# Decode tile with high and low halves in one stationary tile, and layer norms with summed squares on ScalarE

## The reference, cut to what matters

```python
x = _layer_norm(DN_ALPHA * x + 0.5 * _swiglu(x, f1g, f1u, f1d), ln_g[0], ln_b[0])
m, s_new, new_k, new_v = _mixer(x, w_in, w_out, gn_w, sinks, ret_state, k_buf, v_buf)
x = _layer_norm(DN_ALPHA * x + m, ln_g[1], ln_b[1])
x = _layer_norm(DN_ALPHA * x + 0.5 * _swiglu(x, f2g, f2u, f2d), ln_g[2], ln_b[2])
```

## Time and profile before

| | us |
|---|---|
| median of 3 runs | 2297.51 (2296.41 to 2300.42) |
| profiled execution, its own time | 2296.21 |
| its span, first to last instruction | 2294.4 |
| TensorE busy | 2216.7 |
| VectorE busy | 949.5 |
| GpSimd busy | 515.3 |
| ScalarE busy | 452.6 |

### The profile page before, as it was taken

The page is one execution under the profiler, slowest core; times in us unless marked ns, Lnnn a source line. Parts: engine busy times, 40 slices in busy tenths (PEclk is TensorE's granted clock), DMA queues, the critical chain, the costliest instruction groups (busy, mean ns, idle before and its releaser), DMA issues. The chain is left out here.

```text
span 2294.4 us, 31139 instructions
## 1 busy us (share of the span) xinstructions
PE 2216.7 (97%) x12117; PEld 1998.7 (87%) x12117; DVE 949.5 (41%) x1580; ACT 452.6 (20%) x799; POOL 515.3 (22%) x253
## 2 busy tenths in 40 slices
PE   8999999999999989999898899899999999999996
PEld 8999999999999889996676458799999999999995
DVE  5434434344344550012133546634343443434347
ACT  4111111111111221111123540211111111111111
POOL 4121121212212222212122522221212122121213
PEclk9999999999999999999697699999999999999998
DMA  7101011010111011110103030010110101011011
GB/s 267 56 27 55 27 55 53 29 55 27 55 47 45 37 61 65 37 35 17 65 10 138 0 125 1 19 55 28 55 51 31 55 27 55 29 53 55 28 56 78
DMA packets 37817, 118.39 MB, mean 52 GB/s; under 512 B 5879, under 2 KB 10615, under 8 KB 37503
## 3 DMA queue, kind: packets, MB, share of 16 engines
q1 hardware_dynamic: 37759, 117.58, 14.4%
HBM read 106.29 MB, written 11.27 MB: 51 GB/s over the span
## 5 line engine op out<-in xcount | busy, mean ns | idle before, releaser
L111 PE MATMUL bank<-x_hi,f_w_hi 128*128 128x362 f32 (+1 forms) x2104 | 689.3, 328 | 7.7 <-issue 6.4
L113 PE MATMUL bank<-x_hi,f_w_low 128*128 128x362 f32 (+1 forms) x2104 | 689.5, 328 | 0.0
L362 POOL TENSOR_TENSOR f_w_low<-f_w_raw,f_w_hi 128x1024 fp32r<-128x1024 f32 x132 | 316.8, 2414 | 1199.2 <-ACT f_w_hi L288 1199.2
L534 DVE TENSOR_TENSOR acc<-bank,acc 128x512 f32<-128x512 f32 x756 | 500.5, 689 | 15.2 <-PE bank L461 6.9
L514 DVE TENSOR_TENSOR f_h_full<-bank,f_silu 128x362 f32<-128x362 f32 (+1 forms) x132 | 70.7, 536 | 817.4 <-PE bank L113 815.0
L111 PEld LDWEIGHTS bank<-x_hi,f_w_hi 128*128 128x128 f32 x2104 | 396.4, 188 | 10.0 <-issue 8.1
L113 PEld LDWEIGHTS bank<-x_hi,f_w_low 128*128 128x128 f32 x2104 | 396.7, 189 | 0.0
L112 PE MATMUL bank<-x_lo,f_w_hi 128*128 128x362 f32 (+1 forms) x1056 | 346.2, 328 | 0.0
L112 PE MATMUL bank<-x_low,f_w_hi 128*128 128x362 f32 (+1 forms) x1048 | 342.8, 327 | 0.0
L442 PE MATMUL bank<-f_w_hi,f_h_lo 128*128 128x512 f32 x720 | 281.8, 391 | 0.0
L443 PE MATMUL bank<-f_w_low,f_h_hi 128*128 128x512 f32 x720 | 281.5, 391 | 0.0
(11 more groups left out here) (165 smaller groups left out, 2209.9 us busy)
## 6 DMA issues: line engine op xcount, KB each, us to landing
f_w_raw<-ffn_in SPq DMA_DIRECT2D x132, 512.0 KB, 4.5
rp_w_raw<-w_ret_in SPq DMA_DIRECT2D x16, 512.0 KB, 3.5
acc<-x_rows_in SPq DMA_DIRECT2D x2, 2048.0 KB, 11.0
kept_rows<-acc SPq DMA_DIRECT2D x8, 512.0 KB, 2.6
ow_raw<-w_out_in SPq DMA_DIRECT2D x8, 512.0 KB, 11.1
y_out<-acc SPq DMA_DIRECT2D x8, 512.0 KB, 2.6
n_rows<-ln_rows_in SPq DMA_DIRECT2D x6, 512.0 KB, 7.9
gp_stage<-w_att_in SPq DMA_DIRECT2D x6, 512.0 KB, 3.5
```

Of the source, the lines that this page charges most:

```text
L111: pe.matmul(out, wh, xh, start=first, stop=False)
L113: return pe.matmul(out, wl, xh, start=False, stop=last)
L362: pool.tensor_tensor(flat(w_lo[s][j]), flat(w_raw[s][j]), flat(w_hi[s][j]).bitcast(F32), ALU.subtract).then_inc(done, 1)
L534: dve.tensor_tensor(acc[r, t, d], down_ps[(n + 2 * s) % 4][r, :], acc[r, t, d], ALU.add).then_inc(down_free, 1)
```

## The change

**Decode tile in the feed-forward stages.** `h_hi` gets 128 more columns: 64 for the low part of the decode tokens, right behind their high part, and 64 zeros. One stationary tile of 128 columns now holds high and low part, so two matmuls (with the high and the low weights) replace three; the bank's rows 0 to 63 hold the high part's product and rows 64 to 127 the low part's. `acc` keeps both apart in the decode tile over the loop (rows 64 to 127 start at zero), and `last_down` folds them with a matmul by `fold`, two 64x64 identities above each other, in full f32.

**Order.** In `last_down`, the norms and the output projection, the decode tile is the seventh (`ORDER`), and p is a position in that order. `gate_up(B, 1, 2)` comes before `last_down(4)`. `low` of position p - 2 comes right after the mean of p, and three instead of four turns are left for the retention projection.

**Norms.** The last adds also write row sums; VectorE makes the negative mean of two sums; ScalarE squares the shifted tile with a row sum of its own (`deviation`) and takes the root; VectorE adds the negative mean and multiplies by the gain row in one instruction, and multiplies by the reciprocal and adds the bias row in another. GpSimd has no part in the norms.

**Output projection.** The decode tile's halves are copied side by side into `pack`, with 64 zeros behind; the number of matmuls stays. VectorE copies before it frees the banks. `pack` overlaps weights of the second stage, so their first `DOWN` load waits for the products. The retention projection's gate weights wait for the last square.

The diff, cut to its core. Feed-forward stage:

```diff
-        dve.tensor_scalar(acc[DEC:P, BLOCKS, :], acc[DEC:P, BLOCKS, :], 2 * ALPHA, None, ALU.mult).then_inc(scaled, 1)
+        dve.tensor_scalar(acc[0:DEC, BLOCKS, :], acc[0:DEC, BLOCKS, :], 2 * ALPHA, None, ALU.mult).then_inc(scaled, 1)
+        dve.memset(acc[DEC:P, BLOCKS, :], 0.0).then_inc(scaled, 1)
...
-        self.h_hi = [work.put(f"{tag}h_hi{s}", [P, TOK], F32R) for s in range(2)]
-        self.h_lo = [work.put(f"{tag}h_lo{s}", [P, TOK], F32R) for s in range(2)]
+        self.h_hi = [work.put(f"{tag}h_hi{s}", [P, TOK + 2 * DEC], F32R) for s in range(2)]
+        self.h_lo = [work.put(f"{tag}h_lo{s}", [P, SEQ], F32R) for s in range(2)]
...
         if room:
             sp.wait_ge(*room)
+            load_part(sp, 0, 0, DOWN)
...
         silu_and_round(A, 0, 2)
+        norm.high(act, 0)
         norm.deviation(act, 2)
-        norm.high(act, 0)
+        norm.high(act, 1)
         norm.deviation(act, 3)
-        norm.high(act, 1)
-        norm.deviation(act, 4)
         silu_and_round(B, 1, 2)
-        norm.high(act, 2)
-        norm.deviation(act, 5)
-        norm.high(act, 3)
-        norm.deviation(act, 6)
-        norm.high(act, 4)
-        norm.deviation(act, 7)
+        for p in range(4, 8):
+            norm.high(act, p - 2)
+            norm.deviation(act, p)
         norm.deviation(act, 8)
...
-        for t in range(7):
-            norm.gain(pool, t)
...
+        def high_and_low(s):
+
+            return h_hi[s][:, SEQ:SEQ + P], h_hi[s][:, TOK:TOK + P]
...
                     out = down_ps[(n + 2 * s) % 4]
                     hi, lo = flat(w_hi[s][DOWN])[:, d], flat(w_lo[s][DOWN])[:, d]
-                    pe.matmul(out, h_hi[s][:, u], hi, start=True, stop=False)
-                    pe.matmul(out, h_lo[s][:, u], hi, start=False, stop=False)
-                    pe.matmul(out, h_hi[s][:, u], lo, start=False, stop=True).then_inc(down_done, 1)
-
-        def last_down(t):
-
+                    if t == BLOCKS:
+                        both = h_hi[s][:, SEQ:SEQ + P]
+                        pe.matmul(out, both, hi, start=True, stop=False)
+                        pe.matmul(out, both, lo, start=False, stop=True).then_inc(down_done, 1)
+                    else:
+                        pe.matmul(out, h_hi[s][:, u], hi, start=True, stop=False)
+                        pe.matmul(out, h_lo[s][:, u], hi, start=False, stop=False)
+                        pe.matmul(out, h_hi[s][:, u], lo, start=False, stop=True).then_inc(down_done, 1)
...
+
+            t = ORDER[p]
             if t in (0, 2, 5):
...
             if t == 0:
                 pe.wait_ge(down_split, FT)
...
             for half in range(2):
-                n, d = 2 * t + half, slice(512 * half, 512 * half + 512)
+                n, d = 2 * p + half, slice(512 * half, 512 * half + 512)
                 pe.wait_ge(down_free, DOWNS * (A + 1) + n + 1 - 4)
                 out = down_ps[n % 4]
                 for f, s in ((A, 0), (B, 1)):
-                    hi, lo = flat(w_hi[s][DOWN])[:, d], flat(w_lo[s][DOWN])[:, d]
-                    pe.matmul(out, h_hi[s][:, u], hi, start=f == A, stop=False)
-                    pe.matmul(out, h_lo[s][:, u], hi, start=False, stop=False)
-                    mm = pe.matmul(out, h_hi[s][:, u], lo, start=False, stop=f == B)
+                    w_h, w_l = flat(w_hi[s][DOWN])[:, d], flat(w_lo[s][DOWN])[:, d]
+                    if t == BLOCKS:
+                        high, low = high_and_low(s)
+                    else:
+                        high, low = (h[s][:, P * t:P * t + P] for h in (h_hi, h_lo))
+                    pe.matmul(out, high, w_h, start=f == A, stop=False)
+                    if t == BLOCKS and f == A:
+                        pe.matmul(out[0:DEC, :], fold[:, :], acc[:, BLOCKS, d], start=False, stop=False)
+                    pe.matmul(out, low, w_h, start=False, stop=False)
+                    mm = pe.matmul(out, high, w_l, start=False, stop=f == B)
                 mm.then_inc(down_done, 1)
 
         def step(f, s):
...
         norm.turn(pe, 1)
+        gate_up(B, 1, 2)
         last_down(4)
-        gate_up(B, 1, 2)
         norm.turn(pe, 2)
         last_down(5)
         norm.turn(pe, 3)
         last_down(6)
         norm.turn(pe, 4)
         last_down(7)
+        norm.turn(pe, 5)
         last_down(8)
 
...
-                              h_hi[s][:, a:b].bitcast(F32), ALU.subtract).then_inc(h_lo_done, 1)
+            rows = min(b, SEQ)
+            full = h_full[:, buffer_of(f, s, c), :]
+            x = dve.tensor_tensor(h_lo[s][:, a:rows], full[:, 0:rows - a], h_hi[s][:, a:rows].bitcast(F32), ALU.subtract)
+            if b > SEQ:
+                x = dve.tensor_tensor(h_hi[s][:, TOK:TOK + DEC], full[:, SEQ - a:TOK - a],
+                                      h_hi[s][:, SEQ:TOK].bitcast(F32), ALU.subtract)
+            x.then_inc(h_lo_done, 1)
 
...
-            for n in (2 * t, 2 * t + 1):
-                add_part(A, 0, n)
...
-            return down_free, DOWNS * (A + 1) + 2 * t + 2
...
+                dve.wait_ge(down_free, DOWNS * A + n + 1)
+                if t == BLOCKS:
+                    dve.tensor_scalar(acc[0:DEC, t, d], down_ps[n % 4][0:DEC, :], 1.0, 0.0, ALU.mult, ALU.add,
+                                      accum_out=norm.row_sum(p, half)).then_inc(down_free, 1)
+                else:
+                    dve.scalar_tensor_tensor(acc[:, t, d], down_ps[n % 4][:, :], 1.0, acc[:, t, d], ALU.mult, ALU.add,
+                                             accum_out=norm.row_sum(p, half)).then_inc(down_free, 1)
+
+        def added(p):
...
-            if t:
-                norm.shift(dve, t - 1)
-            norm.invert(dve, t)
-            norm.centre(dve, t)
-
+        def norm_tile(p):
+            add_last(p)
+            norm.mean(dve, p, added(p))
+            if 2 <= p <= 7:
+                norm.low(dve, p - 2)
+            if p:
+                norm.centre_and_gain(dve, p - 1)
+                norm.invert(dve, p - 1)
+                norm.shift(dve, p - 1)
+
+        if room:
+            dve.wait_ge(*room)
+        for s in range(2):
+            dve.memset(h_hi[s][:, TOK + DEC:TOK + 2 * DEC].bitcast(F32), 0.0)
         h_and_split(0, 0, 0)
         if first_norm:
             first_norm.low(dve, TOKEN_TILES - 2)
...
         norm_tile(2)
-        norm.low(dve, 0)
         norm_tile(3)
-        norm.low(dve, 1)
-        norm_tile(4)
         h_and_split(B, 1, 2)
-        norm.low(dve, 2)
-        norm_tile(5)
-        norm.low(dve, 3)
-        norm_tile(6)
-        norm.low(dve, 4)
-        norm_tile(7)
-        norm_tile(8)
-        norm.gain(dve, 8)
-        norm.shift(dve, 8)
-        for t in range(5, TOKEN_TILES):
-            norm.low(dve, t)
+        for p in range(4, TOKEN_TILES):
+            norm_tile(p)
+        norm.centre_and_gain(dve, TOKEN_TILES - 1)
+        norm.invert(dve, TOKEN_TILES - 1)
+        norm.shift(dve, TOKEN_TILES - 1)
+        for p in range(6, TOKEN_TILES):
```

New methods of `Norm`, in place of `statistics`, `deviation`, `invert`, `centre`, `gain` and `shift`:

```diff
+    def row_sum(self, p, half):
+        return self.stats[self.part(p), p, half:half + 1]
+
+    def mean(self, dve, p, summed):
+        r = self.part(p)
+        dve.wait_ge(*summed)
+        dve.tensor_scalar(self.stats[r, p, 2:3], self.row_sum(p, 0), self.row_sum(p, 1), -1.0 / D_MODEL,
+                          ALU.add, ALU.mult).then_inc(self.averaged, 1)
+
+    def deviation(self, act, p):
+        r = self.part(p)
+        act.wait_ge(self.averaged, p + 1)
+        act.activation(self.squares[r, :], self.tile(p), ACT.Square, bias=self.stats[r, p, 2:3],
+                       accum_out=self.stats[r, p, 3:4]).then_inc(self.squared, 1)
+        act.wait_ge(self.squared, p + 1)
+        act.activation(self.stats[r, p, 4:5], self.stats[r, p, 3:4], ACT.Sqrt, bias=self.eps[r, 0:1],
+                       scale=1.0 / D_MODEL).then_inc(self.deviated, 1)
+
+    def centre_and_gain(self, dve, p):
+        r = self.part(p)
+        dve.wait_ge(self.rows_loaded, 32)
+        dve.wait_ge(self.squared, p + 1)
+        dve.scalar_tensor_tensor(self.tile(p), self.tile(p), self.stats[r, p, 2:3], self.rows[r, 0, :],
+                                 ALU.add, ALU.mult).then_inc(self.gained, 1)
+
+    def invert(self, dve, p):
+        r = self.part(p)
+        dve.wait_ge(self.deviated, p + 1)
+        dve.reciprocal(self.stats[r, p, 5:6], self.stats[r, p, 4:5]).then_inc(self.inverted, 1)
+
+    def shift(self, dve, p):
+        r = self.part(p)
+        dve.wait_ge(self.inverted, p + 1)
+        dve.wait_ge(self.gained, p + 1)
+        dve.scalar_tensor_tensor(self.tile(p), self.tile(p), self.stats[r, p, 5:6], self.rows[r, 1, :],
+                                 ALU.mult, ALU.add).then_inc(self.affine, 1)
+
+
```

Order, retention projection and output projection:

```diff
+ORDER = (0, 1, 2, 3, 4, 5, BLOCKS, 6, 7)
...
-        for j in (V, GATE):
-            sp.dma_start(w_raw[j][:, :], w_in[j]).then_inc(staged[j], 16)
+        sp.dma_start(w_raw[V][:, :], w_in[V]).then_inc(staged[V], 16)
+        sp.wait_ge(norm.squared, TOKEN_TILES)
```

(51 more changed lines are left out.)

205 lines of the change are left out of this document (92 added, 113 removed).

## The result

The changed kernel took 2275.66 us (median of 6 runs, 2271.29 to 2279.32), the kernel before 2298.55 us beside it (6 runs, 2296.41 to 2300.42): a ratio of 0.9901, 95% interval 0.9886 to 0.9915. The prediction was 2275 us, with a range of 2267 to 2286 us and a chance of 0.85 for faster. The profiled execution of the changed kernel took 2273.8 us (span 2272.0), 22.4 us less than that of the kernel before; the sum had said 21.9.

The account below looks back on a forecast made before the run. TensorE, busy 97% of the span, was taken as the bound, with VectorE setting the pace at the end. Terms -18.4 + 2.4 - 7.2 + 1.3 = -21.9 us gave 2275 us, own range 2270 to 2281, eight in ten 2267 to 2286.

Parts of the forecast that it names:

- the sum: Whole kernel: loop passes -18.4, output projection +2.4, tail -7.2 and first seam +1.3, together -21.9 us.
- Two passes in `down`: Feed-forward loops, decode tile: 80 matmuls go at 0.23 us each, -18.4 us (18.2 to 18.7).
- Start of the output projection: Copies and memsets ahead of freeing the banks cost 1.8 us, a lower clock 0.6: +2.4 us (1.7 to 4.5).
- Tile cost in the norms: VectorE's work on one tile in the norms, from adds to `shift`: 4.1 us a tile.
- The rival of half-rate passes: Norms: `centre_and_gain`, `shift`, perhaps adds take two cycles an element; 2299 us, 2309 with slow adds; chance 0.12.
- Slow accumulation: Norms: only the accumulating adds double, seam +4.2, tail -2.4 us, 2283 us; chance 0.08.
- the loop that doesn't shrink: `down`: another engine sets the pace once TensorE has less, the 18.4 us stay, 2293 us; chance 0.04.
- Tail: Second stage, first `last_down` to VectorE's end: new order and shorter tiles give -7.2 us (-6.4 to -8.1).
- the order's gain: Second stage: `gate_up(B, 1, 2)` ahead of `last_down(4)` makes `h_lo` ready in time, removing TensorE's 3.3 us stall and 0.54 clock.
- First seam: First stage's first `last_down` to the retention projection: +2.3, less 1.0 for transposes moved there: +1.3 us (0 to +3.5).
- ScalarE's chain: End of first seam: square and sqrt precede the `sem_inc` freeing the projection's banks, at 823.7 against 821.4 before.
- the block of transposes: One block (1.0 us) moves from the retention projection into idle time of the first seam.

Follow-up runs that it names:

- the later group: The changed kernel run once more, unchanged, beside three further kernels: 2274.13 us, ratio 0.9905; the kernel before had a median of 2294.58 us there.
- the second move: Kernel with early output-projection banks and `low` behind `shift`, plus the retention projection's four banks freed from TensorE's own start: 2261.93 us, ratio 0.9860.

## Why the prediction was right, point by point

**Two passes in `down`: right.** 80 x 0.23 us = 18.4, measured 18.8 in the two loops before and after, and 18.8 again when a pass was given back.

**Start of the output projection: right, the clock undersized.** Wait +2.1 (predicted 1.8; a copy of 512 elements a row took 0.43 us, not 0.35). The clock did fall, and cost 1.5 us at the least (2.5 when the changed kernel was profiled again), where I took 0.6 within 0 to 2. The kernel with the early `sem_inc` gave back the wait and these 1.5 us. That the line in the table still agrees (+0.5 against +0.6) is luck: the wait at the other end, ahead of the second stage's first matmul, fell by 0.8 us, and the prediction had put that end at nothing, within 0.3.

**Tile cost in the norms: right.** 4.06 us a tile, predicted 4.1. The parts were off both ways: each pass with two SBUF sources 1.20 us start to start instead of 1.08, each accumulating add 0.61 us with its read instead of 0.76, the mean 0.13 instead of 0.2. The rival of half-rate passes is out: the form takes 1.27 us for 1024 f32 elements, against 1.23 for the plain product with the row. The Trainium skill (Vector Engine (DVE) Microarchitecture Reference, section 7) says that this form with two SBUF sources that aren't bf16 has half the throughput; by this trace it has not. Slow accumulation is out too (0.68 us, as without an accumulator), and so is the loop that doesn't shrink.

**Tail: right, for the stated reasons in part.** -7.0 us against -7.2. The prediction had the stall of 3.3 us and the low clock behind it as the order's gain; the run with the order undone shows that the new norms alone would have cut the stall to 1.9 us and kept the clock, so that the order is worth 2 us. Part of the old stall was no matter of order at all: before, the split of the last chunk ran beside GpSimd's gain pass and took 1.58 us, against at most 0.54 us for the 126 splits without GpSimd beside them:

```profile
2263.38 1.58 DVE L520 TENSOR_TENSOR f_h_lo<-f_h_full,f_h_hi 128x362 fp32r<-128x362 f32 x1 [0.57 <-ACT f_h_hi L303]
```

```profile
2262.22 2.35 POOL L666 TENSOR_TENSOR acc<-acc,n_rows 128x1024 f32<-128x1024 f32 x1 [2.37 <-DVE acc L660]
```

**First seam: the step that failed.** Predicted +2.3 us, measured +6.3. The step is the clock, which the prediction priced at the output projection and put at nothing in this seam, and beside it the tile cycle. I had `h_lo` of the last chunk at 796.6 us; on the old time axis it came at 798.4 (788.83 + 9.58), 1.8 us late. TensorE waits 2.2 us for `shift` ahead of the second transposes, and behind that wait it ran at half clock, so that the transposes and the last gate and up products took 1.7 us longer. The kernel with the banks freed early has the same code and the same wait up to there, its clock stayed up, and its `h_lo` ends 32.8 us after the first `last_down`: the prediction's 32.7. The two windows from the start of the transposes, the changed kernel first (third last column: granted clock):

```profile
776.00:780.00 4.00, 3.71 (x16) 3.71 (x17) 2.38 (x7) 1.76 (x2) 0.00 (x0) 0.57 0.32 131
```

```profile
778.00:782.00 4.00, 3.56 (x24) 3.56 (x25) 3.19 (x8) 2.39 (x4) 0.00 (x0) 1.00 0.32 131
```

Of seven profiles with this code and this wait up to there, two show a full clock behind it, and five a half clock that sets in between 0.2 us before and 1.1 us after the end of the wait; what decides between them stays open.

Then I had three tiles at 5.63 us; they took 6.06, 7.64 and 6.06 us, 2.9 more. 1.3 of it are in the cycle of 6.06 us: waits of `low` of 0.77 us instead of 0.45, and longer passes. The rest is the decode tile at half clock. Together 4.7, less 0.5 in the last tile and ScalarE's chain. So some 3.2 of the 4.0 us missed are the clock's in this profile. The run that moves `low` shows that its place matters for both: the cycle falls to 5.2 us, TensorE's wait ahead of the second transposes to 1.25 us, and the clock stays up until the wait at the end of the seam.

**What made up for it.** -5.1 us instead of -1.0 in stages that the change doesn't touch, but for the block of transposes. The retention projection, which has one block less, is 0.8 us shorter. The attention stage, word for word the same, gives 4.6 us. Its duration alone is no sign of the change: the kernel with the early banks has the changed kernel's code there and took 125.1 us in it, as the kernel before. But that kernel was faster in the stages ahead of it, and the whole stretch took 525.4 to 529.7 us in all twelve profiles of changed kernels, against 533.2 in the only profile of the kernel before. The medians point the same way: the measured parts with a middle of -1.0 would give -18.3 us, where the medians are 22.9 us apart (19.5 to 26.2) and in the later group 20.5 (18.1 to 25.7). So some gain in the middle may well belong to the change; no run shows by what, and one profile of the kernel before can't tell it from chance. For the prediction it is luck either way: it has no term for this gain, and its total was right to 0.5 us because a loss of 4 us that it didn't see met a gain of 4 us that it didn't see.

## What to carry to other kernels

Work taken off the bounding engine inside a loop can be counted pass by pass; what an order on another engine costs at a seam can't, until each in-order wait is followed from the first tile on, and each wait of TensorE that comes out of it is priced with half clock behind it as well: here one wait of 2.2 us cost 1.7 us more in some executions and nothing in others. A semaphore that only says "free" belongs ahead of any work that its waiter doesn't need, and on the waiter's own engine if that one already waits for the true condition: the two such moves here took 3.6 us off the start of the output projection and 4.3 us off the first seam, where the waits that they took away were 2.1 and 4.1 us. The matmuls behind the gap gained 1.5 and 1.6 us by a higher clock, and the second move lost 2.3 us to a wait that came back later. When a total agrees, cut both traces into stretches before believing the parts.
